# The opening of the first FFN of a two-block transformer kernel: loads and splits by two feature tiles, norm factor behind the third weight unit

## The reference, cut to what matters

```python
def rmsnorm(x, g):
    xf = x.astype(jnp.float32)
    y = xf * lax.rsqrt(jnp.mean(xf * xf, axis=-1, keepdims=True) + RMS_EPS)
    return (y * g.astype(jnp.float32)).astype(x.dtype)

def swiglu(h, w_gate, w_up, w_down):
    return (jax.nn.silu(h @ w_gate) * (h @ w_up)) @ w_down

x = x + 0.5 * swiglu(rmsnorm(x, norm_ffn1[l]), w_ffn1_gate[l], w_ffn1_up[l], w_ffn1_down[l])
# then the hybrid mixer, a second FFN, the final norm, and a second block of depth 2 with
# four more FFNs, an RWKV mixer and a stick-breaking mixer
```

## Time and profile before

| what | value |
|---|---|
| time, median of 3 runs | 1576.3 us (1575.78 to 1580.74) |
| the profiled execution's own time | 1576.25 us |
| its span, first to last instruction | 1575.0 us |
| PE busy | 98% |
| weight loads of PE busy | 86% |
| DVE / ACT / POOL busy | 67% / 55% / 9% |
| mean granted clock of PE | 0.999 of full speed |
| DMA, mean rate | 181 GB/s |

### The profile page before, as it was taken

One profiled execution on the slowest core, in us unless ns is written; L12 is line 12 of the kernel. 1 busy time (PEld: TensorE's weight loads), 2 busy tenths in 40 slices (PEclk: granted clock), 3 DMA queues, 4 the chain that ended last, 5 costly groups with the idle time before them and its releaser, 6 DMA issues.

```text
span 1575.0 us, 26453 instructions
## 1 busy us (share of the span) xinstructions
PE 1548.2 (98%) x11126; PEld 1349.7 (86%) x11126; DVE 1055.0 (67%) x1526; ACT 868.4 (55%) x1279; POOL 138.3 (9%) x139
## 2 busy tenths in 40 slices
PE   8999999999999999999998999999999999999998
PEld 7888898688888988889988888889888888898886
DVE  5766676866666665667966776657766676786566
ACT  6555555655555555556743365555655565665553
POOL 0001020000000010002663001000100010001000
PEclk9999999999999999999999999999999999999999
DMA  8878555346555565555300365553755552555651
GB/s 300 265 237 277 203 186 216 109 173 226 179 187 193 172 216 192 187 187 194 134 4 31 135 241 186 188 201 137 251 195 183 187 185 83 166 208 187 206 174 76
DMA packets 42806, 285.68 MB, mean 181 GB/s; under 512 B 5162, under 2 KB 5162, under 8 KB 11072
## 3 DMA queue, kind: packets, MB, share of 16 engines
q1 hardware_dynamic: 39456, 272.81, 49.7%
q0 software_dynamic: 3232, 11.18, 2.7%
HBM read 278.21 MB, written 5.24 MB: 180 GB/s over the span
## 4 chain that ended last, share of the span: by engine, by line
PE 87%; DVE 6%; ACT 3%; DMA 2%; issue 1%; SPq 0%; DVEq 0%; ACTq 0%
PE P L255 85%; DVE wlo L243 2%; PE P L266 2%; DMA raw<-ws 2%; ACT whi L229 1%; DVE AR L1750 0%; DVE AR L1881 0%; PE P L2279 0%; DVE AR L1896 0%; DVE AR L1894 0%; ACT AR L1733 0%; DVE AR L1887 0%; DVE AR L2388 0%; DVE AR L2380 0%; DVE AR L1884 0%
## 5 line engine op out<-in xcount | busy, mean ns | idle before, releaser
L255 PE MATMUL P<-xt,whi 128*128 128x512 f32 (+1 forms) x3216 | 717.5, 347 | 6.6 <-DVE wlo L243 2.2
L255 PEld LDWEIGHTS P<-xt,whi 128*128 128x128 f32 x3216 | 550.9, 190 | 77.6 <-issue 7.2
L243 DVE TENSOR_TENSOR wlo<-raw,whi 128x2048 fp32r<-128x2048 f32 x243 | 554.7, 2288 | 57.7 <-PE P L255 49.0
L229 ACT ACTIVATE whi<-raw 128x2048 fp32r<-128x2048 f32 x243 | 464.0, 1910 | 130.2 <-PE P L255 87.8
L255 PE MATMUL P<-xt,wlo 128*128 128x256 f32 x2544 | 434.4, 282 | 0.0
L255 PEld LDWEIGHTS P<-xt,wlo 128*128 128x128 f32 x2544 | 383.6, 191 | 17.9
L649 DVE SCALAR_TENSOR_TENSOR AR<-P,AR 128x256 f32<-128x256 f32 x228 | 96.4, 423 | 227.3 <-ACT AR L642 227.2
L255 PE MATMUL P<-whi,hh 128*128 128x512 f32 x504 | 197.6, 392 | 0.5 <-DVE wlo L243 0.5
L255 PE MATMUL P<-wlo,hh 128*128 128x512 f32 x504 | 196.8, 390 | 0.0
L255 PE MATMUL P<-whi,hl 128*128 128x512 f32 x504 | 196.1, 389 | 0.0
L642 ACT ACTIVATE AR<-P 128x256 f32<-128x256 f32 x228 | 86.0, 377 | 118.3 <-PE P L255 118.3
(11 more groups left out here) (253 smaller groups left out, 1042.3 us busy)
## 6 DMA issues: line engine op xcount, KB each, us to landing
raw<-ws SPq DMA_DIRECT2D x247, 1024.0 KB, 4.9
gb<-gains SPq DMA_DIRECT2D x13, 512.0 KB, 7.2
by_distance<-AR POOLq DMA_DIRECT2D x16, 256.0 KB, 5.0
raw<-ws SPq DMA_DIRECT2D x4, 512.0 KB, 7.7
AR<-by_distance POOLq DMA_DIRECT2D x4, 512.0 KB, 5.5
AR<-by_distance POOLq DMA_DIRECT2D x2, 768.0 KB, 6.6
x<-x_in SPq DMA_DIRECT2D x2, 512.0 KB, 8.5
AR<-mem_in POOLq DMA_DIRECT2D x1, 1024.0 KB, 5.3
```

What stands on the lines that cost most here:

```text
L229: act.e.activation(k.whi[n % NHI][:, :], k.raw[raw_slot(u)][:, :], ACT.Copy).then_inc(*k.s_hi.inc(u))
L243: dve.e.tensor_tensor(k.wlo[n % NLO][:, :], k.raw[raw_slot(u)][:, :], k.whi[n % NHI][:, :].bitcast(F32), ALU.subtract).then_inc(*k.s_lo.in ...
L255: return pe.e.matmul(o, l, r, start=start, stop=stop, skip_group_check=True)
```

## The change

Five things are altered, all in the first FFN:

1. SP loads x's columns in four DMAs of two feature tiles, each followed by a DMA that brings the same two feature tiles of both halves of unit 0 (two pieces of 1 KiB in each partition). The two halves of unit 1 and unit 2 follow, and the two token DMAs of x come last.
2. ACT and DVE split in the same order: two tiles of x, then the matching 512 columns of unit 0, four times; then unit 1 by halves, each in one instruction; unit 2; then the squares; then the high part of unit 3; only then the root and the Silu table. DVE makes the low part of unit 2 ahead of the variance, the reciprocal and the diagonals.
3. PE warms up with 10 products instead of 18, does unit 0 by pairs of feature tiles with the low products of the pair before, and turns the norm factor into `RROW`'s source between the high and the low products of unit 2 instead of unit 1.
4. `ffn_scalar`: ACT looks ahead three units for n = 0, 1, 2 too.
5. `ffn_vector`: for n = 0 DVE looks ahead three units, so it makes the low part of unit 3 ahead of the first sums.

```diff
@@ ffn_scalar
-            hi_to(k, act, u + (2 if t == "f1" and n < 3 else 3))
+            hi_to(k, act, u + 3)
@@ ffn_vector
-            lo_to(k, dve, u + 2)
+            lo_to(k, dve, u + (3 if t == "f1" and n == 0 else 2))
@@ sync_program
-    sp.e.dma_start(k.XCOL[:, 0:1032], k.x_col[:, 0:1032]).then_inc(*k.s_col[0].inc(by=16))
-    sp.e.dma_start(k.XCOL[:, 1032:2056], k.x_col[:, 1032:2056]).then_inc(*k.s_col[1].inc(by=16))
-    part(0, 0)
-    part(0, 1)
-    tokens(0)
-    part(1, 0)
-    tokens(1)
-    part(1, 1)
+    def columns(g):
+        w = slice(512 * g + (8 if g else 0), 512 * g + 520)
+        sp.e.dma_start(k.XCOL[:, w], k.x_col[:, w]).then_inc(*k.s_col[g].inc(by=16))
+    def first_part(g):
+        w = slice(256 * g, 256 * g + 256)
+        sp.e.dma_start(begin_half(k.raw[0])[:, :, w], begin_half(k.ws[0, :, :])[:, :, w]).then_inc(*k.s_part[0][g].inc(by=16))
+    for g in range(4):
+        columns(g)
+        first_part(g)
+    for s in range(2):
+        part(s)
     load_units(k, sp, 2, NRAW)
+    for a in range(2):
+        tokens(a)
@@ begin_tensor (new)
+    warm_tensor(k, pe)                      # 10 products, were 18
+    for g in range(4):
+        pe.wait_ge(*k.s_hi.after("part", 0, g))
+        for c in (2 * g, 2 * g + 1):
+            pe.wait_ge(*k.s_xl.after("f1", c))
+            for s in range(2):
+                begin_high(k, pe, 0, s, c)
+        if g:
+            lows(g - 1)
+    lows(3).then_inc(*k.s_used.inc(0))
+    distances_tensor(k, pe)
+    ... high and low products of unit 1, then the high products of unit 2
+    for a in range(2):
+        pe.wait_ge(*k.s_dv.after("diag", a))
+        last = mm(pe, k.P[7][:, 128 * a:128 * a + 128], k.ONE, k.DIAG[:, a, :])
+    last.then_inc(*k.s_pe.inc("rrow"))
+    pe.wait_ge(*k.s_lo.after(2))
+    ... low products of unit 2
@@ begin_scalar (new)
+    for g in range(4):
+        high(2 * g)
+        high(2 * g + 1)
+        w = slice(256 * g, 256 * g + 256)
+        act.wait_ge(*k.s_part[0][g].after())
+        act.e.activation(begin_half(k.whi[0])[:, :, w], begin_half(k.raw[0])[:, :, w],
+                         ACT.Copy).then_inc(*k.s_hi.inc("part", 0, g))
+    ... unit 1 by halves
+    act.hi = U_FFN1 + 2
+    hi_to(k, act, U_FFN1 + 2)
     square(0)
     square(1)
+    hi_to(k, act, U_FFN1 + 3)
     act.wait_ge(*k.s_var.after("f1"))
     act.e.activation(k.sm[:, 6:8], k.sm[:, 10:12], ACT.Sqrt).then_inc(*k.s_rt.inc("f1"))
     act.e.activation(k.sm[:, 31:32], k.sm[:, 30:31], ACT.Silu)
@@ begin_vector (new)
+    for g in range(4):
+        low_columns(2 * g)
+        low_columns(2 * g + 1)
+        ... low part of the same 512 columns of unit 0
+    ... unit 1 by halves
+    distances_vector(k, dve)
+    dve.lo = U_FFN1 + 2
+    lo_to(k, dve, U_FFN1 + 2)
     ... variance, reciprocal, diagonals, half, as before
```

More of the change, by code:

```diff
@@ L162, in tiles_and_signals @@
     k.s_gn = [sig("gn0"), sig("gn1")]
-    k.s_col = [sig("col0"), sig("col1")]
-    k.s_part = [[sig(f"part{u}{s}") for s in range(2)] for u in range(2)]
+    k.s_col = [sig(f"col{g}") for g in range(4)]
+    k.s_part = [[sig(f"part{u}{n}") for n in range(4 - 2 * u)] for u in range(2)]
     k.s_id, k.s_vec, k.s_cst, k.s_base, k.s_rel = (
@@ L3120, in tokens, with part @@
         sp.e.dma_start(k.x[:, a, :], k.x_in[a * 128:(a + 1) * 128, :]).then_inc(*k.s_x[a].inc(by=16))
[L3122 to L3133 removed]
+    def columns(g):
[4 more added lines that the diff above has]
+        sp.e.dma_start(begin_half(k.raw[0])[:, :, w], begin_half(k.ws[0, :, :])[:, :, w]).then_inc(*k.s_part[0][g].inc(by=16))
+    def part(s):
+        w = slice(1024 * s, 1024 * s + 1024)
+        sp.e.dma_start(k.raw[1][:, w], k.ws[1, :, w]).then_inc(*k.s_part[1][s].inc(by=16))
+    for g in range(4):
[3 more added lines that the diff above has]
+        part(s)
     load_units(k, sp, 2, NRAW)
+    for a in range(2):
+        tokens(a)
     def gains(name, rows_, after):
@@ L3210, in norms, with begin_half @@
     }
-def begin_high_tensor(k, pe, u, s):
-    wh, _ = weights(k, u)
[L3216 to L3226, removed]
+def begin_half(t):
+    return (t if len(t.shape) == 2 else t[:, :, :]).rearrange("p (s n) -> p s n", s=2)
@@ L3228, in begin_low_tensor, with begin_slot, begin_high, begin_low @@
+def begin_slot(s, c):
+    return slice((s * 8 + c) * 128, (s * 8 + c) * 128 + 128)
+def begin_high(k, pe, u, s, c):
+    wh, _ = weights(k, u)
+    return mm(pe, k.P[LEAD_BANKS[u][s]][:, :], wh[:, begin_slot(s, c)],
+              k.xt[:, c, :, :, :].rearrange("p a s t -> p (a s t)"), c == 0, False)
+def begin_low(k, pe, u, s, c):
     _, wl = weights(k, u)
     own, _ = lead_parts(k, u, s)
[L3230 to L3233, removed]
@@ L3234, in begin_low_tensor, with lows @@
-    return last
+    return mm(pe, own, wl[:, begin_slot(s, c)], k.xt[:, c, :, 0, :], False, c == 7)
 def warm_tensor(k, pe):
     pe.wait_ge(*k.s_po.after("one"))
-    for n in range(18):
+    for n in range(10):
         mm(pe, k.P[7][:, 0:128], k.ONE, k.ONE)
 def begin_tensor(k, pe):
-    warm_tensor(k, pe)
[L3247 to L3258, removed]
+    def lows(g):
+        pe.wait_ge(*(k.s_lo.after("part", 0, g) if g < 3 else k.s_lo.after(0)))
+        for c in (2 * g, 2 * g + 1):
+            for s in range(2):
+                last = begin_low(k, pe, 0, s, c)
+        return last
@@ new lines, in begin_tensor @@
+    warm_tensor(k, pe)
+    for g in range(4):
+        pe.wait_ge(*k.s_hi.after("part", 0, g))
+        for c in (2 * g, 2 * g + 1):
+            pe.wait_ge(*k.s_xl.after("f1", c))
+            for s in range(2):
+                begin_high(k, pe, 0, s, c)
[3 more added lines that the diff above has]
+    distances_tensor(k, pe)
+    for s in range(2):
+        pe.wait_ge(*k.s_hi.after("part", 1, s))
+        for c in range(8):
+            begin_high(k, pe, 1, s, c)
@@ new lines, in begin_tensor @@
+    for s in range(2):
+        pe.wait_ge(*(k.s_lo.after(1) if s else k.s_lo.after("part", 1)))
+        for c in range(8):
+            last = begin_low(k, pe, 1, s, c)
+    last.then_inc(*k.s_used.inc(1))
+    pe.wait_ge(*k.s_hi.after(2))
+    for s in range(2):
+        for c in range(8):
+            begin_high(k, pe, 2, s, c)
+    for a in range(2):
+        pe.wait_ge(*k.s_dv.after("diag", a))
+        last = mm(pe, k.P[7][:, 128 * a:128 * a + 128], k.ONE, k.DIAG[:, a, :])
+    last.then_inc(*k.s_pe.inc("rrow"))
@@ L3259, in begin_tensor @@
+    pe.wait_ge(*k.s_lo.after(2))
+    for s in range(2):
+        for c in range(8):
+            last = begin_low(k, pe, 2, s, c)
+    last.then_inc(*k.s_used.inc(2))
     pe.wait_ge(*k.s_ev.after("dist"))
@@ L3267, in high @@
     def high(c):
-        act.wait_ge(*k.s_col[c // 4].after())
+        act.wait_ge(*k.s_col[c // 2].after())
         act.wait_ge(*k.s_col[0].after())
@@ L3271, in high @@
                          scale=k.GCOL[:, c:c + 1]).then_inc(*k.s_xh.inc("f1", c))
[L3273 to L3276, removed]
     def square(a):
@@ L3281, in square @@
                          accum_out=k.sm[:, 4 + a:5 + a]).then_inc(*k.s_sq.inc("f1", a))
[L3283 to L3290, removed]
+    for g in range(4):
[5 more added lines that the diff above has]
+                         ACT.Copy).then_inc(*k.s_hi.inc("part", 0, g))
+    for s in range(2):
+        w = slice(1024 * s, 1024 * s + 1024)
+        act.wait_ge(*k.s_part[1][s].after())
+        act.e.activation(k.whi[1][:, w], k.raw[1][:, w], ACT.Copy).then_inc(*k.s_hi.inc("part", 1, s))
+    act.hi = U_FFN1 + 2
+    hi_to(k, act, U_FFN1 + 2)
     square(0)
-    part(1, 0, 0, 2)
     square(1)
-    part(1, 1, 0, 2)
+    hi_to(k, act, U_FFN1 + 3)
     act.wait_ge(*k.s_var.after("f1"))
@@ L3305, in begin_vector, with low_columns @@
     dve.e.memset(k.sm[:, 30:31], 1.0).then_inc(*k.s_dv.inc("one"))
[L3307 to L3313, removed]
+    def low_columns(c):
         dve.wait_ge(*k.s_xh.after("f1", c))
@@ L3317, in begin_vector @@
                                    op1=ALU.subtract).then_inc(*k.s_xl.inc("f1", c))
-    low(0, 0)
-    low(0, 1)
-    low(1, 0)
+    for g in range(4):
+        low_columns(2 * g)
+        low_columns(2 * g + 1)
+        w = slice(256 * g, 256 * g + 256)
+        dve.wait_ge(*k.s_hi.after("part", 0, g))
+        dve.e.tensor_tensor(begin_half(k.wlo[0])[:, :, w], begin_half(k.raw[0])[:, :, w], begin_half(k.whi[0])[:, :, w].bitcast(F32),
+                            ALU.subtract).then_inc(*(k.s_lo.inc("part", 0, g) if g < 3 else k.s_lo.inc(0)))
+    for s in range(2):
+        w = slice(1024 * s, 1024 * s + 1024)
+        dve.wait_ge(*k.s_hi.after("part", 1, s))
+        dve.e.tensor_tensor(k.wlo[1][:, w], k.raw[1][:, w], k.whi[1][:, w].bitcast(F32),
+                            ALU.subtract).then_inc(*(k.s_lo.inc(1) if s else k.s_lo.inc("part", 1)))
+    distances_vector(k, dve)
+    dve.lo = U_FFN1 + 2
+    lo_to(k, dve, U_FFN1 + 2)
     for a in range(2):
```

6 lines of the change are left out of this document (removed).

## The result

The changed kernel takes 1585.1 us (median of 5 runs, 1583.5 to 1588.1); the kernel before took 1576.3 beside it (5 runs, 1575.6 to 1580.7). The ratio is 1.0052, with a 95% interval of 1.0041 to 1.0063: slower by 0.5%, some 8 us, where 1.75 us faster was forecast. Over the later sessions the kernel before has a median of 1578.2 to 1578.8 in 25 to 27 runs; each experiment is compared with the runs beside it. One run of the kernel before (3881.8 us) and one of warm10_late (3077.4 us) were slow ones, over a thousand us above the rest, and are in no ratio.

What follows compares the result with a forecast made beforehand. Up to unit 5's start at 41.67 us the DVE and ACT chain was taken to bound, then PE. Chain 2.19 us less, landing 0.45 later: net about 1.75, 1576.25 to 1574.5 us; 8-in-10 range 1573.2 to 1576.9.

Steps and rivals of the forecast that it cites:

- I cost the rest at nothing: Everything behind unit 5: claimed to cost 0 us, at worst giving back the 1.75 us gain.
- that cover: After unit 5: PE never idle to 190 us, with DVE busy 41.19 and ACT 32.32 of 58.33 us.
- my rivals: Clock falls, 1576.1 (0.17); packets at upper bound, 1575.85 (0.12); only PE counts, 1570.7 (0.04); nothing lasts, 1576.25 (0.07).
- those of 2.7 and 1.8: PE's waits before: 2.7 us in three waits for a low part, 1.8 for the first high parts.
- unit 5 itself: Start of unit 5 on PE in the first FFN: 39.95 instead of 41.67, 1.72 us earlier.
- Eight warm-up products less cost nothing as long as the clock has risen.: Opening on PE: shorter warm-up costs 0; unit 0 starts near 5.5 and ends near 11.6 instead of 14.5.
- 0.8 us ahead of the norm factor's diagonals: Unit 2 on PE: high products end about 21.8, diagonals ready at 22.6.
- The landing of unit 3: Load of unit 3: lands at 19.8 instead of 19.35, 0.45 us later through 1024 more packets.
- my 5 and 28: Cost per extra packet in ns, lower and upper bound: 0.35 and 1.8 us in all over 16 engines.
- The chain to d0: DVE and ACT turns from unit 3's landing: first sum of g0 at 24.8, d0 at 34.35 instead of 35.23.
- The clock in the gap: Rival: PE idle 3.5 us ahead of d0, its clock falls, 1576.1 us; chance 0.17, of it 0.06 slower than before.
- the 1.6 estimated: Loss in us if d0 begins at 1.2 GHz for about 3.2 us, half of that lost.

Runs made afterwards that it cites:

- warm10_late: Kernel before with 10 warm-up products instead of 18 and the one weight load issued near 860 us held back about 2 us; 1585.3 us, ratio 1.0042.
- after_warm18: Changed kernel with the old 18 warm-up products instead of 10; 1579.3 us, ratio 1.0008.
- before_warm10: Kernel before with 10 warm-up products instead of 18, nothing else; 1587.0 us, ratio 1.0055.
- again: Changed kernel once more, unaltered, for a second trace; 1586.4 us, one run.
- fill8: Changed kernel with 8 added products of ones in PE's gap between unit 3 and d0; 1577.4 us, ratio 0.9990.
- warm10_pad: Kernel before with 10 warm-up products and 8 products of ones added ahead of unit 8 of the first FFN; 1582.1 us, ratio 1.0026.
- ahead_warm18: Changed kernel with units 4 to 6 split one step earlier and 18 warm-up products; 1578.0 us, ratio 1.0002.
- look_only: Kernel before with only the two look-ahead edits on ACT and DVE; 1575.9 us, ratio 0.9987.
- fill16: Changed kernel with 16 added products of ones in PE's gap between unit 3 and d0; 1578.3 us, ratio 0.9996.
- ahead: Changed kernel with the splits of units 4, 5 and 6 one step earlier, 10 warm-up products kept; 1582.6 us, ratio 1.0022.
- before_late: Kernel before with one weight load of the RWKV chain held back by 2 us; 1579.9 us, ratio 1.0011.

## Why the prediction was wrong

**The sign and the size.** "I cost the rest at nothing; if that cover were gone, the 1.75 would be given back, no more" is the step that failed. I took the rest of the program as a rigid block behind unit 5, since PE showed no idle time to 190 us. It isn't rigid: a block of PE's program comes at a fixed instruction, a load at a fixed event, and both share the DMA engines. Taking 32 instructions out ahead of everything shifted the first against the second. In the RWKV chain PE then waited for a block behind a load, in the FFNs for a load that had a block in its flight. Some six of the 8 us are that (after_warm18 against the changed kernel), and before_warm10 shows that it needs nothing else of the change. None of my rivals had it, and the row was on the page, in the queue named instruction and in the waits put down to "issue" in the trace of before: with 2.3 us they were the second largest kind, and I named those of 2.7 and 1.8 as the longest two.
The second step that failed is unit 5 itself: 39.95 predicted, 43.62 measured. Of these 3.67 us, 0.84 are the later start of d0 and 2.83 its slow clock, as follows.
The same section of the Trainium skill's Runtime page calls the cost of crossing into the next block "mostly hidden". In the FFNs no trace here shows PE waiting for a block, but the load that has the block in its flight lands 1.2 us later; in the stage of small products the measurements differ: waits of 0.4 to 2.99 us, all six of 2.3 us and more with a 1 MiB load's whole data passing just ahead of the block.

**"Eight warm-up products less cost nothing as long as the clock has risen."** The condition failed. The first eight products of unit 0 took 3.8 us from start to start of what follows, 0.47 us each, twice the 0.23 of a product at the higher level. In again and fill8 the clock had risen near 5.2 and fell back within unit 0, behind its first four products: the stretch 8.5 to 12 us of fill8 shows 0.51. So unit 0 ended at 14.0 instead of 11.6; its start, at 6.14 and not at 5.5, is 0.6 of that. PE, which I had 0.8 us ahead of the norm factor's diagonals, was now 1.2 behind them: they were there at 23.2, and the factor's products started at 24.33. In before_warm10 the same cut costs 1.2 us at unit 5, and in warm10_pad and warm10_late 2.3 and 2.6.

**The landing of unit 3.** Predicted 19.8, bounds 19.35 to 21.15, measured 20.37 (issued at 11.57, 8.8 us to landing). The 1.0 us over the old landing is 16 ns for each of the 1024 additional packets over 16 engines, between my 5 and 28, if it is put on the packets alone; the value was a factor of two low, the range held it in this trace. It doesn't hold all: with the new order unit 3 lands at 20.3 to 21.1 in the five traces with 10 warm-up products, but at 22.4 and 21.8 in the two with 18 (after_warm18, ahead_warm18); with the old order it is 19.3 to 20.2 in all seven. The bound of 28 ns was too low by its own rows: 12 to 16 us held 328 packets where pieces of 8 KiB make 211, so the 0.94 us stand against some 330 packets more, not 530; that is 45 ns each, 2.9 us in all.

**The chain to d0.** First sum of g0 at 24.8 predicted, 25.66 measured: 0.57 from the landing and 0.3 from the late factor. From there to the start of d0 I had 9.5 us, and it took 9.53. d0 at 35.19 was 0.84 late for these two reasons alone. The wait ahead of it is 2.75 (3.5 predicted, as unit 3 was later too). look_only agrees with the same chain within 0.3 us. From the first sum to d0 it is 9.52 us in again, fill8 and after_warm18 too, so this part of the reading holds. What scatters is the first sum itself: 25.66 in the first trace of the changed kernel, 26.56 to 27.38 in these three.

**The clock in the gap.** It was the rival with 0.17, and it happened in both traces of the changed kernel and in that of after_warm18; with the gap filled (fill8, fill16) or closed (ahead) it did not. Its price was 2.9 us in the first trace of the changed kernel, where nearly all of d0 ran slowly (8.43 us against the 5.57 of fill8), and 1.5 and 1.4 us in again and after_warm18 (7.06 and 6.98), near the 1.6 estimated. The error was to hold the lack of such a gap in the old trace for evidence that the clock would stay up. There was no row on waits above 1.6 us, in either direction. The rule of the Trainium skill (TensorE: Matmul & The Clock Gate, Part 1: The HAM clock gate), that an idle stretch may put the clock back, is what the traces show: waits of 2.75 and 3.45 us ahead of d0 were followed by 0.43 us a product, waits of up to 1.02 ahead of d0 were not. Elsewhere the length of the wait alone doesn't tell: in look_only the clock fell behind a wait of 1.39 us at 862, in warm10_late it didn't behind one of 2.32 at 869.

**What became of the gain.** Without the shorter warm-up the change is at 1.0008 (0.9998 to 1.0018), and the two look-ahead edits alone are at 0.9987. So no gain of the new loads and the late norm factor shows: they brought PE earlier to a point (unit 3 at 26.7 instead of 28.86) at which it waits for DVE, and the longer wait cost the clock. The part of the change that works is the part that shortens DVE's and ACT's turn.

**What stays open.** Why the wait for a low part near 225 comes and goes: 0.5 us or more of it is there in all kernels with 10 products and nothing added ahead of it, also in warm10_pad, where the program's position was put right ahead of it. In five of these six a block falls within the flight of a load there (6.0 to 6.3 us instead of 4.8 to 5.0); in warm10_pad none does. The loads land later there beside POOL's transfers, but no run isolates it. That a block delays the loads ahead of 353, 1298 and 1410 is read from fourteen traces, and that the waits vanish with the position is measured; no run moved one of these loads alone. How much of the later landing of unit 3 is the size of the packets and how much the order of the loads is open too, and so is what sets off the slow stretch near 300.

## What to carry to other kernels

A cut of a few instructions at the start of a long unrolled program isn't local: it moves the points at which the program itself is reloaded against the data loads. When a result is off in stages that were not touched, compare the starts of the same instruction in both traces, look for waits put down to "issue" beside packets of the instruction queue and for loads that take longer from issue to landing, and run the old kernel with only the instruction count changed before explaining anything else. And an engine brought earlier to a wait that stays has a longer wait: on PE that can cost the clock of the work behind it, so close the gap or fill it.

## What the runs showed of the hardware

- A block of PE's program of 16 KiB waits behind a 1 MiB load in flight (3.3 us of data), and PE stood for up to 2.99 us; with small products PE uses up a block in 3.5 to 4.3 us. Held back by 2 us, one such load made PE's wait grow from 0.95 to 2.87 us.
- The other way round, a 1 MiB load with such a block in its flight lands after 6.06 us in the median, and after 4.85 without (141 and 1643 loads of fourteen traces).
- Behind waits of 2.66 to 3.45 us PE's clock fell to the lower level for a few us: in both traces of the changed kernel at d0 and near 867, in before_warm10 near 868, in after_warm18 at d0, in ahead and before_late near 864. It fell behind 1.39 us in look_only, and not behind 2.32 us in warm10_late. Ten warm-up products (the last at about 5 us) and a wait of 0.5 to 3.5 us ahead of unit 0 left it low for 3 to 6 us in unit 0.
- In a stretch of small products near 300 us the clock falls in some executions and not in others (0.53 against 1.00); the delay grew by 1.3 to 2.8 us over it.
- With pieces of 1 and 2 KiB instead of 4 KiB, and a new order of the loads, unit 3 landed 1.0 us later in the first pair of traces, 16 ns for each of 1024 packets more over 16 engines; over seven traces of each order it is 20.3 to 22.4 against 19.3 to 20.2 us.
